# A decoder trunk on one core: memory transposed before its norm scale, dummy products while TensorE waits, and the last scaling and store in halves

## What is computed

```python
def rmsnorm(x, gain):
    y = x32 * lax.rsqrt(jnp.mean(x32 * x32, axis=-1, keepdims=True) + EPS)
    return (y * gain).astype(x.dtype)

mem_n = rmsnorm(mem, mem_norm_gain)
for l in range(DEPTH):
    h = rmsnorm(x, norm_gain[l])
    ...
    mkv = (mem_n @ w_mem_kv[l]).reshape(B, MEM_TOKENS, 2, MEM_HEADS, HEAD_DIM)
    o_c = memory_attention(c_q.reshape(B, S, MEM_HEADS, HEAD_DIM), mkv[:, :, 0], mkv[:, :, 1])
    ...
    x = x + mixed @ w_out[l]
return rmsnorm(x, final_norm_gain)
```

## Time and profile before

| | |
|---|---|
| runs, us | 758.89, 759.11, 759.40 |
| median, us | 759.11 |
| profiled execution, span | 759.2 us, 14735 instructions |
| profiled execution, time given beside its span | none; the span stands for it |
| TensorE busy | 736.1 us, 97% |
| VectorE busy | 447.7 us, 59% |
| ScalarE busy | 389.1 us, 51% |
| GpSimd busy | 226.5 us, 30% |

### The profile page before, as it was taken

The page is one execution under the profiler, slowest core; times in us unless marked ns, Lnnn a source line. Parts: engine busy times, 40 slices in busy tenths (PEclk is TensorE's granted clock), DMA queues, the critical chain, the costliest instruction groups (busy, mean ns, idle before and its releaser), DMA issues.

```text
span 759.2 us, 14735 instructions
## 1 busy us (share of the span) xinstructions
PE 736.1 (97%) x5672; PEld 701.0 (92%) x5672; DVE 447.7 (59%) x652; ACT 389.1 (51%) x725; POOL 226.5 (30%) x194
## 2 busy tenths in 40 slices
PE   4999999999999999999999999999999999999986
PEld 4999998999998898899999999899999889889976
DVE  4756568566755555455555566766566555446543
ACT  5745446445565565343445534654556555553333
POOL 4128543560100000155210774257110000013542
PEclk9999999999999999999999999999999999999999
DMA  8955557654443443465775554675543434335541
GB/s 325 348 169 174 166 172 244 197 190 142 139 118 105 127 152 106 145 177 175 261 260 168 172 177 161 212 235 170 179 142 112 146 109 129 118 115 175 177 145 57
DMA packets 34704, 128.88 MB, mean 170 GB/s; under 512 B 4016, under 2 KB 4048, under 8 KB 34128
## 3 DMA queue, kind: packets, MB, share of 16 engines
q1 hardware_dynamic: 34256, 127.43, 52.2%
q10 hardware_dynamic: 384, 0.56, 0.2%
HBM read 124.83 MB, written 3.15 MB: 169 GB/s over the span
## 4 chain that ended last, share of the span: by engine, by line
PE 87%; POOL 4%; issue 3%; DVE 2%; ACT 2%; DMA 1%; DVEq 0%; POOLq 0%; ACTq 0%
PE pj L377 24%; PE pj L378 23%; PE pj L379 23%; PE pv L579 3%; POOL mix L1294 2%; PE tr L553 2%; PE pv L582 1%; POOL mix L1296 1%; PE sc L377 1%; PE sc L379 1%; PE sc L378 1%; PE sc L527 1%; PE sc L533 1%; POOL gates L1277 1%; DVE mix L946 1%
## 5 line engine op out<-in xcount | busy, mean ns | idle before, releaser
L866 DVE TENSOR_TENSOR w_lo<-raw,w_hi 128x1024 fp32r<-128x1024 f32 x224 | 302.1, 1353 | 223.5 <-ACT w_hi L648 221.9
L648 ACT ACTIVATE w_hi<-raw 128x1024 fp32r<-128x1024 f32 x224 | 236.2, 1059 | 211.3 <-PE pj L379 200.0
L377 PE MATMUL pj<-h_hi,w_hi 128*128 128x256 f32 x1024 | 293.6, 287 | 0.0
L379 PE MATMUL pj<-h_lo,w_hi 128*128 128x256 f32 x1024 | 289.6, 283 | 0.0
L378 PE MATMUL pj<-h_hi,w_lo 128*128 128x256 f32 x1024 | 289.6, 283 | 0.0
L377 PEld LDWEIGHTS pj<-h_hi,w_hi 128*128 128x128 f32 x1024 | 196.3, 192 | 2.5 <-DVE w_lo L866 1.5
L378 PEld LDWEIGHTS pj<-h_hi,w_lo 128*128 128x128 f32 x1024 | 196.4, 192 | 0.1
L379 PEld LDWEIGHTS pj<-h_lo,w_hi 128*128 128x128 f32 x1024 | 196.2, 192 | 0.0
L1288 POOL TENSOR_TENSOR o_lo<-ot,o_hi 128x256 fp32r<-128x256 f32 (+1 forms) x16 | 16.7, 1042 | 271.8 <-ACT o_hi L748 271.8
L377 PE MATMUL pj<-w_hi,h_hi 128*128 128x256 f32 x256 | 73.7, 288 | 5.9 <-DVE mix L949 4.4
L377 PE MATMUL pj<-o_hi,w_hi 128*128 128x256 f32 x256 | 73.6, 288 | 0.5 <-DVE o_lo L890 0.5
(11 more groups left out here) (219 smaller groups left out, 1029.0 us busy)
## 6 DMA issues: line engine op xcount, KB each, us to landing
raw<-in_stream SPq DMA_DIRECT2D x224, 512.0 KB, 3.5
lnb<-in_rows SPq DMA_DIRECT2D x2, 768.0 KB, 7.1
pars<-in_par SPq DMA_DIRECT2D x2, 516.0 KB, 5.2
xs<-in_x SPq DMA_DIRECT2D x1, 1024.0 KB, 10.6
memory_hi<-o_hi SPq DMA_DIRECT2D x1, 1024.0 KB, 6.6
memory_lo<-o_lo SPq DMA_DIRECT2D x1, 1024.0 KB, 8.7
o_hi<-memory_hi SPq DMA_DIRECT2D x1, 1024.0 KB, 5.4
o_lo<-memory_lo SPq DMA_DIRECT2D x1, 1024.0 KB, 7.6
```

The costliest lines, as they stand in the source:

```text
L377: pe.matmul(dst, a_hi, b_hi, start=first, stop=False, skip_group_check=True)
L379: return pe.matmul(dst, a_hi, b_lo, start=False, stop=last, skip_group_check=True)
L648: act.activation(w_hi[:, c % SPL, :], raw[:, c % RAW, :], ACT.Copy).then_inc(hi_done, 1)
L866: dve.tensor_tensor(w_lo[:, c % SPL, :], raw[:, c % RAW, :], w_hi[:, c % SPL, :].bitcast(F32), ALU.subtract).then_inc(lo_done, 1)
```

## The change

The memory tiles are transposed as they arrive, with the gain but without the row scale. The scale goes in behind the projections: for MV (tokens on partitions) as the scale of ScalarE's copies, for MK (tokens along the row) as a product with a broadcast row on VectorE. That row is made by TensorE from two diagonals. Twelve products of the identity with itself, into a bank not yet in use, stand ahead of the transposes. The last scaling of each tile is done half by VectorE and half by ScalarE, and each half stored by itself. The DMA scratch is made smaller, which gives room to the new tensors.

```diff
+WARM = 12
-COPIED = ("MK", "MV", "KC", "VC", "KS", "KW", "VS", "VW", "AV", "AU", "Q", "CQ")
+COPIED = ("MV", "KC", "VC", "KS", "KW", "VS", "VW", "AV", "AU", "Q", "CQ")
...
             for t in range(2):
-                sp.wait_ge(fin[t], 1)
-                sp.dma_start(out[t * P:(t + 1) * P, :], xn[:, t, :]).then_inc(out_done, 16)
+                sp.wait_ge(fin_dve, t + 1)
+                sp.dma_start(out[t * P:(t + 1) * P, 0:D // 2], xn[:, t, 0:D // 2]).then_inc(out_done, 16)
...
                 if n == 0:
                     pe.wait_ge(consts, 2)
+                    for i in range(WARM):
+                        pe.matmul(pv[:, 0:P], ident[:, :], ident[:, :], start=True, stop=True)
...
-                    pe.wait_ge(xn_ready, 2 * n + t + 1)
+                    if n == 0:
+                        pe.wait_ge(mem_in[t], 16)
+                    else:
+                        pe.wait_ge(xn_ready, 2 * (n - 1) + t + 1)
...
+            def rstd_row():
+
+                pe.wait_ge(diagr_ready, 2)
+                for t in range(2):
+                    mm = pe.matmul(mi[:, P * t:P * t + P], ones[:, :], diagr[:, t, :], start=True, stop=True)
+                mm.then_inc(rrow_mm, 1)
...
                     work(l, b, 0)
+                    if l == 0 and b == AT["MK0"]:
+                        rstd_row()
...
-                    act.wait_ge(xn_ready, 2)
+                    act.wait_ge(summed, 2)
...
-                    if k == "MK" or k == "MV":
+                    if k == "MV":
                         after(act, pv_done, NPV * l)
+                        act.wait_ge(rstd_ready, 2)
+                        i = 256 * (b - AT["MV0"])
+                        for t in range(2):
+                            ins = act.activation(mv[:, t, i:i + 256], pj[b % 2][:, 256 * t:256 * t + 256], ACT.Copy,
+                                                 scale=rstd_m[:, t:t + 1])
+                        ins.then_inc(copied, 1)
+                        return
...
-            act.wait_ge(const_step, 5)
+            act.wait_ge(const_step, 6)
             act.activation(sums[:, 0, 0:2], minus_half[:, :], ACT.Square)
             act.dma_start(rc[:, :], rot_consts).then_inc(consts_in, 16)
             act.dma_start(pos, positions.to_broadcast([ROT, S])).then_inc(consts_in, 16)
+            split(0)
+            act.wait_ge(consts_in, 48)
+            norm_hi(0, o_hi, mgain)
+            split(1)
             act.wait_ge(consts, 1)
             square(0, mems)
-            split(0)
-            split(1)
-            act.wait_ge(consts_in, 48)
-            norm_hi(0, o_hi, mgain)
             for c in range(2, LEAD):
                 split(c)
...
-                if t == 0:
-                    act.wait_ge(gained, 4)
-                    act.wait_ge(rstd_ready, 2 * (DEPTH + 1) + 1)
-                    act.activation(xn[:, 0, :], xn[:, 0, :], ACT.Copy, scale=rstd[:, 0:1]).then_inc(fin[0], 1)
+                act.wait_ge(gained, 4 + t)
+                act.wait_ge(rstd_ready, 2 * (DEPTH + 1) + t + 1)
+                act.activation(xn[:, t, D // 2:], xn[:, t, D // 2:], ACT.Copy, scale=rstd[:, t:t + 1]).then_inc(fin_act, 1)
+                act.wait_ge(fin_act, t + 1)
+                act.dma_start(out[t * P:(t + 1) * P, D // 2:], xn[:, t, D // 2:]).then_inc(out_done, 16)
...
+            def rstd_diagonal():
+
+                for t in range(2):
+                    dve.wait_ge(rstd_ready, t + 1)
+                    dve.wait_ge(consts, 2)
+                    dve.tensor_scalar(diagr[:, t, :], ident[:, :], rstd_m[:, t:t + 1], None, ALU.mult)\
+                       .then_inc(diagr_ready, 1)
+
+            def memory_keys(l, b):
+
+                i = b - AT["MK0"]
+                wait_block(dve, l, b)
+                after(dve, pv_done, NPV * l)
+                if l == 0 and i == 0:
+                    dve.wait_ge(rrow_mm, 1)
+                    dve.tensor_copy(rrow[:, :], mi[:, 0:S]).then_inc(rrow_ready, 1)
+                    dve.wait_ge(rrow_ready, 1)
+                dve.tensor_tensor(mk[:, 2 * i:2 * i + 2, :], bank_view(b),
+                                  rrow[:, :].unsqueeze(1).to_broadcast([P, 2, S]), ALU.mult).then_inc(mk_ready, 1)
...
+            split(0)
+            norm_lo(0, o_hi, o_lo, mgain)
+            split(1)
             row_sums(0)
-            normalise(0, mems, mems)
-            split(0)
-            split(1)
-            norm_lo(0, o_hi, o_lo, mgain)
             for c in range(2, LEAD):
                 split(c)
+            rstd_diagonal()
...
                     split(c + LEAD)
+                    if b > 0 and KIND[b - 1] == "MK":
+                        memory_keys(l, b - 1)
...
-            dve.tensor_scalar(xn[:, 1, :], xn[:, 1, :], rstd[:, 1:2], None, ALU.mult).then_inc(fin[1], 1)
+                dve.wait_ge(gained, 4 + t)
+                dve.wait_ge(rstd_ready, 2 * (DEPTH + 1) + t + 1)
+                dve.tensor_scalar(xn[:, t, 0:D // 2], xn[:, t, 0:D // 2], rstd[:, t:t + 1], None, ALU.mult)\
+                   .then_inc(fin_dve, 1)
...
+            pool.memset(ones[:, :], 1.0).then_inc(const_step, 1)
             pool.memset(sq[:, :, :], 0.0).then_inc(consts, 1)
...
-    nc = bacc.Bacc("TRN2", target_bir_lowering=False, num_devices=1)
+    nc = bacc.Bacc("TRN2", target_bir_lowering=False, num_devices=1, dynamic_dma_scratch_size=4096)
```

More of the change, by code:

```diff
@@ L190, in trunk @@
         rstd = sb("rstd", [P, 2])
+        rstd_m = sb("rstd_m", [P, 2])
+        ones = sb("ones", [P, P])
+        diagr = sb("diagr", [P, 2, P])
+        rrow = sb("rrow", [P, S])
         minus_half = sb("minus_half", [P, 2])
@@ L214, in trunk @@
         summed, squares, rstd_ready, xn_ready = sem("summed"), sem("squares"), sem("rstd_ready"), sem("xn_ready")
+        diagr_ready, rrow_mm, rrow_ready, mk_ready = map(sem, ("diagr_ready", "rrow_mm", "rrow_ready", "mk_ready"))
         h_tr, h_hi_done, h_lo_done = sem("h_tr"), sem("h_hi_done"), sem("h_lo_done")
@@ L231, in trunk @@
         mix_prod, mix_add, mix_hi, mix_lo = sem("mix_prod"), sem("mix_add"), sem("mix_hi"), sem("mix_lo")
-        x_added, gained, fin = sem("x_added"), sem("gained"), [sem("fin0"), sem("fin1")]
+        x_added, gained, fin_act, fin_dve = map(sem, ("x_added", "gained", "fin_act", "fin_dve"))
         last_done, last_added = sem("last_done"), sem("last_added")
@@ L262, in wait_evacuated @@
             k, name = KIND[p], BLOCKS[p]
-            if k in COPIED:
+            if k == "MK":
+                eng.wait_ge(mk_ready, 2 * l + p - AT["MK0"] + 1)
+            elif k in COPIED:
                 eng.wait_ge(copied, n_copied(l, name))
@@ L367, in _ @@
             for t in range(2):
-                sp.wait_ge(fin[t], 1)
-                sp.dma_start(out[t * P:(t + 1) * P, :], xn[:, t, :]).then_inc(out_done, 16)
+                sp.wait_ge(fin_dve, t + 1)
+                sp.dma_start(out[t * P:(t + 1) * P, 0:D // 2], xn[:, t, 0:D // 2]).then_inc(out_done, 16)
             sp.wait_ge(memory_out, 32)
-            sp.wait_ge(out_done, 32)
+            sp.wait_ge(out_done, 64)
         @block.tensor
@@ L850, in _ @@
                                accum_out=sq[:, t, 3:4]).then_inc(squares, 1)
-                if t == 0:
-                    act.wait_ge(gained, 4)
-                    act.wait_ge(rstd_ready, 2 * (DEPTH + 1) + 1)
-                    act.activation(xn[:, 0, :], xn[:, 0, :], ACT.Copy, scale=rstd[:, 0:1]).then_inc(fin[0], 1)
+                act.wait_ge(gained, 4 + t)
[3 more added lines that the diff above has]
+                act.dma_start(out[t * P:(t + 1) * P, D // 2:], xn[:, t, D // 2:]).then_inc(out_done, 16)
+            act.wait_ge(out_done, 64)
         @block.vector
@@ L1140, in _ @@
                 dve.tensor_reduce(ss[:, t:t + 1], sq[:, t, :], AX.X, ALU.add).then_inc(summed, 1)
-            dve.wait_ge(gained, 5)
-            dve.wait_ge(rstd_ready, 2 * (DEPTH + 2))
-            dve.tensor_scalar(xn[:, 1, :], xn[:, 1, :], rstd[:, 1:2], None, ALU.mult).then_inc(fin[1], 1)
+                dve.wait_ge(gained, 4 + t)
+                dve.wait_ge(rstd_ready, 2 * (DEPTH + 1) + t + 1)
+                dve.tensor_scalar(xn[:, t, 0:D // 2], xn[:, t, 0:D // 2], rstd[:, t:t + 1], None, ALU.mult)\
+                   .then_inc(fin_dve, 1)
         @block.gpsimd
@@ L1151, in inverse_root @@
                     pool.wait_ge(summed, 2 * n + e)
-                    after(pool, xn_ready, 2 * n)
+                    after(pool, xn_ready, 2 * (n - 1))
+                    root = rstd if n else rstd_m
                     pool.tensor_scalar(ss[:, t:e], ss[:, t:e], 1.0 / D, EPS, ALU.mult, ALU.add)\
@@ L1155, in inverse_root @@
                     pool.wait_ge(mean_sq, 2 * n + e)
-                    pool.tensor_tensor(rstd[:, t:e], ss[:, t:e], minus_half[:, t:e], ALU.pow)\
+                    pool.tensor_tensor(root[:, t:e], ss[:, t:e], minus_half[:, t:e], ALU.pow)\
                         .then_inc(rstd_ready, e - t)
@@ L1207, in _ @@
```

(7 more changed lines are left out.)

## The result

The changed kernel takes 762.89 us (762.60 to 763.13, 5 runs) where the kernel before took 759.11; the ratio is 1.0041, 95% interval 1.0028 to 1.0053. It is slower, as forecast, but by 3.8 us between the medians and not 1.8, and its median lies 0.3 us above the range. The ratio, which takes all runs together, makes the difference 2.1 to 4.0 us.) The profiled execution of the changed kernel has a span of 760.9, only 1.7 above the 759.2 of the profile before. These two differences, 1.7 in the spans and 3.8 in the times, are what had to be explained.

The account below looks back on a forecast made before the run. TensorE, busy 97% of the span, was taken as the bound, with time won or lost only where it is not fed. Plus 2.1 at chunk 1's end, minus 0.3 in the tail: plus 1.8, 761.0 us; range 758.6 to 762.6.

Parts of the forecast that it names:

- N, the gain copies: Prologue: ScalarE's start N, 9.0 or 9.9 against 11.51 before; 9.0 taken, about 2.5 us won.
- The row in TensorE's queue: Before chunk 1: TensorE waits for VectorE's diagonals until 18.0, standing still at least 2.4 us.
- The clock after the stop: Row and chunk 1: cold restart, chance 0.65, 16 products at 0.21; chunk 1 ends at 23.1, 2.1 later.
- The rule on transposes: Prologue: transposes do not count as busy TensorE, so the dummies' warmth is not held and chunk 0 starts cold.
- The tail: Last scaling and stores: halves go out 0.1 to 0.3 earlier; bounds 0.1 to 0.7, 0.3 us taken as gain.
- The estimate of at most 0.6: Tail stores: with a fixed part of about 2.0 us, the two halves land at most 0.6 us earlier.
- What else moves: Middle: refills, late masks, VectorE evacuations and MV copies lie in existing waits; uncovered, they cost some 4 us.
- the band of 762 to 765: Rival: something of the middle surfaces, the two VectorE evacuations or the late masks; chance 0.05.
- the base of the sum: Whole kernel: profiled span 759.2, within 0.1 of median 759.11, so the median moves by the same plus 1.8.
- one number: the end of chunk 1, 21.0 before: Prologue: judged by chunk 1's end alone, as no new wait shows after it; forecast 23.1.
- The faster rival: Before chunk 1: row ready when TensorE arrives, chunk 1 starts 2.5 to 3.6 earlier; 755.2 to 756.3, chance 0.11.

Follow-up runs that it names:

- row_after_chunk2: Changed kernel with the scaling row's two products behind chunk 2 instead of chunk 0 in TensorE's queue; 761.08 us, ratio to before 1.0010.
- stop_filled: Changed kernel with 16 more dummy products between chunk 0 and the scaling row; 760.84 us, ratio to before 1.0014.
- best_no_dummies: `row_late_masks_angles` without the 12 dummy products; 758.25 us, ratio to before 0.9979.
- no_dummies: Changed kernel without the 12 dummy products ahead of the transposes; 763.27 us, ratio to before 1.0041.
- before_again: The kernel before, unchanged, run once more for a second profile; 759.67 us.
- old_tail: Changed kernel with the tail of before, one scaling of 1024 columns and one store per token tile; 763.43 us, ratio to before 1.0042.
- row_late_masks_first: Changed kernel with the scaling row behind chunk 2 and GpSimd's masks ahead of memory's roots; 758.22 us, ratio to before 0.9986.
- row_late_masks_angles: `row_late_masks_first` with the rope angles one block later, behind the second keys; 757.58 us, ratio to before 0.9976.

## Why the prediction was right, and where not

- **N, the gain copies.** Forecast 9.0 with the positions as the last wait; measured 9.04, by that wait.
- **The row in TensorE's queue.** Row at 18.0, stop of 2.4 to 4 us; measured 17.75 and 3.93, released by the diagonal. The chain of ScalarE's and VectorE's order held within 0.3 us, and `row_after_chunk2` shows that this wait decided.
- **The clock after the stop.** Forecast cold with 0.65, 2.1 later at chunk 1's end; measured 1.64 later, as 12 and not 16 slow products came before the rise. `stop_filled` puts the clock's part at 1.4 to 1.5. Right in kind, too large by 0.46.
- **The rule on transposes.** I wrote that the trace agreed with the Trainium skill's page "TensorE: Matmul & The Clock Gate" (Part 4: PE-mode transpose), by which transposes do not count. It does not hold in every execution: in `best_no_dummies` the spacing fell from 0.21 to 0.11 at 8.7 with nothing but transposes since 5.77, and in the changed kernel chunk 0 was fast after 1.9 us of transposes and an idle 1.0. In `no_dummies` the same transposes brought no rise until 15.2, and in the three profiles of the kernel before none either. Sixteen transposes without a rise were too thin for that sentence. The sum did not rest on it.
- **The tail.** Forecast 0.3, measured 0.07. The mis-sized term is ScalarE's half: 0.6 by the rate of a split, measured 0.72, and its store took 2.5. The estimate of at most 0.6 beside that term was worked out from a figure for transfers that GpSimd issues, and these stores are issued by SyncE and ScalarE; nothing here tests it.
- **What else moves.** Right that none of it showed in the changed kernel; but it was the next wait, and I had given it no more than 0.05 and no order. With the stop gone, the late masks cost 1.9 us and a slow stretch. The measured 762.89 lies in the band of 762 to 765 that I gave this case, but by coincidence: in the changed kernel's profile no stop follows the first one in the middle.
- **The step that failed** is the base of the sum: "the profiled span is 759.2, within 0.1 of the median 759.11, so the median moves by the same", and with it "one number: the end of chunk 1, 21.0 before". The time holds about 1.7 us outside the span, and the profile before was of a slower execution, 1.8 above the median; in `before_again` the split behind chunk 1 starts 1.17 earlier. Against its own profile the forecast of plus 1.8 measured plus 1.7, in part by luck, since the clock term was 0.46 too large and the tail term 0.23. Against `before_again` the changed kernel's split starts 2.81 later and its span is 3.0 longer. The forecast's span of 761.0 should have been set against 757.4 (759.1 less 1.7), which makes plus 3.6 where 3.8 was measured. The changed kernel shows one group only (762.6 to 763.1 in five runs). That fits its stop: an early rise in chunk 0 is lost again, as the clock fell behind the stop in all three profiles that have it open, those of the changed kernel, `old_tail` and `no_dummies`.
- The faster rival, 755.2 to 756.3, is what the changed kernel becomes when its condition is made true: `row_late_masks_first`, span 755.8.

## What to carry to other kernels

When an operand's scale is moved behind its use, put what makes the scale where its consumer needs it, not where it is first thought of: an in-order engine waits for it with everything that is ready behind. After removing such a stop, list the next latest producer on each engine before pricing the gain. And a span from one profile is no median: compare span with span, and ask from which group of executions the profile comes. Two versions whose profiles agree can still differ in most of their executions, as `row_late_masks_first` and `row_late_masks_angles` do.

## What the runs showed that was not expected

- Three profiles of the kernel before, 759.2, 757.9 and (with the small scratch) 759.4, differ almost only by when the clock rose: after 4.2, 1.9 and 5.0 us of products.
- The same four fold selects on GpSimd took 1.28 us when VectorE had nothing to do and ScalarE only its table load, 3.19 before and 3.90 beside VectorE's splits in `row_after_chunk2`.
- At the end of layer 0 the fall of the clock costs nothing: the second chunk after the stop starts 4.57 us behind the first with the fall (362.09 to 366.66) and 4.58 without it in `before_again` (360.86 to 365.44). Without the fall TensorE stands 1.47 us before it, released by GpSimd's `h_lo`; with the fall the slow products fill that wait.
